# The high parts of the normed queries and keys are copied by GpSimd in place of ScalarE

## The reference

```
def rmsnorm(x, g):
    y = x32 * lax.rsqrt(jnp.mean(x32 * x32, axis=-1, keepdims=True) + NORM_EPS)
    return (y * g.astype(jnp.float32)).astype(x.dtype)
q = rmsnorm(split_heads(q, NSA_HEADS), q_g)         # NSA queries; keys ks, kw with k_g[1], k_g[2]
q = rmsnorm(split_heads(q, FOX_HEADS), q_g)         # FOX queries
k = rmsnorm(split_heads(k, FOX_HEADS), k_g)         # FOX keys
```

## Time and profile before

| | |
|---|---|
| median of 3 runs | 457.0 us (453.78 to 457.54) |
| the profiled execution, device time | 457.69 us |
| its span, first to last instruction | 455.9 us |
| busy: PE, DVE, ACT, POOL | 431.8, 297.0, 254.8, 74.4 us |
| mean granted TensorE clock | 0.981 of full speed |

### The profile page before, as it was taken

How to read it: one execution, slowest core, us unless ns; L and a number is a source line. 1 busy time by engine, 2 the same in 40 slices (tenths; PEclk the granted TensorE clock), 3 DMA queues, 4 the chain that set the end, 5 groups by cost and what they waited for, 6 DMA issues and landing times.

```text
span 455.9 us, 6481 instructions
## 1 busy us (share of the span) xinstructions
PE 431.8 (95%) x2205; PEld 332.8 (73%) x2205; DVE 297.0 (65%) x632; ACT 254.8 (56%) x500; POOL 74.4 (16%) x122
## 2 busy tenths in 40 slices
PE   5899999999589979999999999999799999999997
PEld 1477777878568866676667897888577778888885
DVE  5975569878858998767427873757886448722204
ACT  5645694766635577878618884852576635311100
POOL 4002240000000036666400000000166300000000
PEclk9899999999978999999999999999999999999999
DMA  7822404432041210000011224371400013832004
GB/s 250 330 92 93 128 13 126 109 99 93 0 138 48 92 47 3 1 1 1 1 46 48 93 74 158 103 214 55 138 2 1 1 46 106 294 110 92 0 1 184
DMA packets 12961, 39.15 MB, mean 86 GB/s; under 512 B 1792, under 2 KB 2048, under 8 KB 12672
## 3 DMA queue, kind: packets, MB, share of 16 engines
q1 hardware_dynamic: 12928, 38.73, 25.9%
HBM read 32.43 MB, written 2.10 MB: 76 GB/s over the span
## 4 chain that ended last, share of the span: by engine, by line
PE 79%; DVE 9%; ACT 6%; issue 3%; DMA 1%; SPq 1%; POOL 0%; DVEq 0%; ACTq 0%
PE bank L1185 11%; PE bank L1187 11%; PE bank L1186 11%; PE bank L1299 6%; PE bank L1280 6%; PE bank L1402 5%; PE bank L1400 5%; PE bank L1401 5%; PE bank L1271 3%; PE bank L1272 3%; PE bank L1196 2%; PE bank L1166 2%; PE bank L1215 2%; PE bank L1167 2%; PE bank L1168 2%
## 5 line engine op out<-in xcount | busy, mean ns | idle before, releaser
L1185 PE MATMUL bank<-xh,wh 128*128 128x512 f32 x256 | 110.0, 430 | 4.9 <-DVE wl L818 4.9
L1187 PE MATMUL bank<-xh,wl 128*128 128x512 f32 x256 | 102.0, 398 | 0.0
L1186 PE MATMUL bank<-xl,wh 128*128 128x512 f32 x256 | 101.4, 396 | 0.0
L818 DVE TENSOR_TENSOR wl<-raw,wh 128x1024 fp32r<-128x1024 f32 (+1 forms) x51 | 61.0, 1204 | 30.4 <-ACT wh L527 30.1
L527 ACT ACTIVATE wh<-raw 128x1024 fp32r<-128x1024 f32 (+1 forms) x51 | 52.3, 1036 | 30.2 <-PE bank L1402 29.6
L1185 PEld LDWEIGHTS bank<-xh,wh 128*128 128x128 f32 x256 | 49.2, 192 | 19.1 <-issue 9.7
L1186 PEld LDWEIGHTS bank<-xl,wh 128*128 128x128 f32 x256 | 49.0, 191 | 13.8 <-issue 4.0
L1187 PEld LDWEIGHTS bank<-xh,wl 128*128 128x128 f32 x256 | 49.0, 191 | 11.3
L1023 DVE CUSTOM_DVE_ANT_0 bank<-bank,mask_row 128x256 f32<-128x256 f32 (+3 forms) x96 | 46.7, 499 | 13.7 <-PE bank L1272 12.7
L490 POOL TENSOR_SCALAR probs<-probs,rcp,gates 128x384 f32<-128x384 f32 (+3 forms) x44 | 27.0, 624 | 118.1 <-DVE rcp L1039 118.0
L1402 PE MATMUL bank<-wh,yl 128*128 128x512 f32 x96 | 37.8, 394 | 0.0
(11 more groups left out here) (211 smaller groups left out, 782.3 us busy)
## 6 DMA issues: line engine op xcount, KB each, us to landing
raw<-in_w_in SPq DMA_DIRECT2D x36, 512.0 KB, 3.5
raw<-in_w_out SPq DMA_DIRECT2D x12, 512.0 KB, 3.4
x_raw<-in_xT SPq DMA_DIRECT2D x8, 256.0 KB, 5.9
x_res<-in_x_tok SPq DMA_DIRECT2D x1, 2048.0 KB, 9.4
out_y<-y_out SPq DMA_DIRECT2D x8, 256.0 KB, 2.1
raw<-in_w_in SPq DMA_DIRECT2D x3, 384.0 KB, 3.0
cmp_w_sb<-in_cmp_w SPq DMA_DIRECT2D x1, 1024.0 KB, 10.6
kh_fox<-kh_fox SPq DMA_DIRECT2D x8, 128.0 KB, 2.3
```

The costliest lines, as they stand in the source:

```text
L818: dve.tensor_tensor(wl[:, c % HL, cols], raw[:, c % RAW, cols], wh[:, c % HL, cols].bitcast(F32), ALU.subtract).then_inc(wl_ready, 1)
L1185: pe.matmul(dst, hi, xh[:, k, :], start=(k == 0), stop=False)
L1186: pe.matmul(dst, hi, xl[:, k, :], start=False, stop=False)
L1187: mm = pe.matmul(dst, lo, xh[:, k, :], start=False, stop=(k == KT - 1))
```

## The change

The 28 copies of high parts (two for each of the 14 normed chunks) leave ACT's queue and enter GpSimd's, from the same source to the same place. Each copy on GpSimd waits for `normed` of its chunk, for the recurrence's work on GpSimd, from fq 0 on for the 64 NSA scalings, and for the copy before it (`h_ready`). GpSimd's queue is written anew: the eight multiplications, the copies of the 6 chunks of NSA, the 64 scalings of NSA, the copies of the 8 chunks of FOX, the scalings of FOX. DVE's, PE's and SP's queues are unchanged, and wait for the same semaphores.

```diff
+            def norm_high(c):
+                kind, j = CHUNKS[c]
+                n = nth_normed(c)
+                pool.wait_ge(normed, n + 1)
+                if kind == "fq" and j == 0:
+                    pool.wait_ge(s_ready, NSA_UNITS)
+                for s in range(2):
+                    high, _ = operand_parts(c, s)
+                    pool.wait_ge(lru_ixs, LRU_T)
+                    if c >= NORMED[6]:
+                        pool.wait_ge(p_scaled, NSA_UNITS)
+                    if 2 * n + s:
+                        pool.wait_ge(h_ready, 2 * n + s)
+                    nc.gpsimd.tensor_copy(high, qr[half_of(s), n % 2, :]).then_inc(h_ready, 1)
...
+            for j in range(LRU_T):
+                pool.wait_ge(lru_sig, 2 * j + 2)
+                nc.gpsimd.tensor_tensor(ig[:, j, :], ig[:, j, :], xc[:, j, :], ALU.mult).then_inc(lru_ix, 1)
+            for j in range(LRU_T):
+                pool.wait_ge(lru_sqrt, j + 1)
+                pool.wait_ge(lru_ix, j + 1)
+                nc.gpsimd.tensor_tensor(ig[:, j, :], ig[:, j, :], u_pad[:, j, 0:SEQ], ALU.mult).then_inc(lru_ixs, 1)
+            for c in NORMED[0:6]:
+                norm_high(c)
+            pool.wait_ge(gates_ready, 1)
+            pool.wait_ge(h_ready, 12)
+            scale_probs(0, NSA_UNITS)
+            for c in NORMED[6:]:
+                norm_high(c)
+            pool.wait_ge(h_ready, 2 * len(NORMED))
+            scale_probs(NSA_UNITS, UNITS)
...
-            def norm_high(c):
...
-                        act.activation(high, qr[half_of(s), n % 2, :], ACT.Copy).then_inc(h_ready, 1)
...
-                    norm_high(c - 1)
...
-                norm_high(c - 1)
```

More of the change, by code:

```diff
@@ L491, in scale_probs @@
                                             ALU.mult, ALU.mult).then_inc(p_scaled, 1)
-            pool.wait_ge(small_consts, 1)
[L494 to L510, removed]
+            def norm_high(c):
[12 more added lines that the diff above has]
+                    nc.gpsimd.tensor_copy(high, qr[half_of(s), n % 2, :]).then_inc(h_ready, 1)
```

## The result

The changed kernel takes 460.77 us (median of 4 runs, 459.59 to 462.41) against 457.02 us (4 runs, 453.78 to 457.54): a ratio of 1.0095, 95% interval 1.0054 to 1.0136, or 2.5 to 6.2 us. The forecast was 461.6 us with a range of 457.0 to 467.0. The profiled execution took 459.59 us with a span of 457.4 us, against 457.69 and 455.9 us before.

The account below looks back on a forecast made before the run. The prediction took TensorE's matmuls as most of the time and DVE's queue as the bound up to zl 0; 3.93 us (NSA) plus 0.70 us (FOX) on the 457.0 us median gave 461.6 us, range 457.0 to 467 us.

Parts of the forecast that it names:

- The bound: From the norms of the NSA queries up to zl 0, DVE's queue bounds; it idles only 1.65 us in all there.
- ACT's relief is worth nothing: Taking 28 copies, 17.6 us, off ACT gains at most 0.37 us at the seeds for nq 2; counted at nothing.
- The copy: One GpSimd copy of 512 columns takes 0.65 us (0.52 to 0.77), bounded from memset, scaling and two-tensor product rows.
- The turns: GpSimd's second copy and DVE's first low part can't run at once, so the second low part starts 0.77 us later.
- rival 1: Second copy and first low part overlap, being on different partitions; 457.7 us, no difference; chance 0.19.
- d: Extra DVE time per normed chunk: 0.16 + 0.77 = 0.93 us, from 0.67 to 1.17 us with the copy's duration.
- The NSA stage: Six chunks delay DVE's queue before zl 0, less 1.65 us idle: zl 0 starts 3.93 us later (2.4 to 5.4).
- The FOX stage: Read-out of fk 0 comes 2.16 us late against 1.46 us slack before its square's mean: PE stalls 0.70 us.
- The clock: PE's restart at zl 0 may fall better or worse against the clock grant: 1.7 us either way, nothing in the sum.
- The sum: 3.93 + 0.70 = 4.6 us added to the 457.0 us median: 461.6 us, 1.0% slower.
- 2: Rival: the GpSimd copy is slow, 1.04 us or more, costing 11.6 us together: 468.6 us; chance 0.13.
- 3: Rival: faster, with memset-short copies, no turns and PE's restart sparing the half-clock slices: about 452 us; chance 0.04.

Follow-up runs that it names:

- the run without the chain: Changed kernel, but the second GpSimd copy of each chunk raises its own semaphore and no longer waits for the first's h_ready; one execution, 460.24 us.

## Why the prediction was right, and where it was off

**The bound.** Right. DVE's queue up to zl 0 was what the change lengthened, and a slip put into the old kernel brought PE's waits back at vn 2 and zl 0. The prediction missed two more idle spells of that queue, 0.60 us at 112.58 and 0.16 us at 115.18, both behind ACT ("nothing else"); they keep their length in the changed kernel, so they absorbed nothing and the sum isn't hurt.

**ACT's relief is worth nothing.** Right as far as these runs can tell: half of the copies off ACT without a turn gave 0.9981, with an interval that holds 1, and in the changed kernel PE gains more than 0.1 us nowhere but in half-clock stretches.

**The copy.** 0.65 us was taken, from 0.52 to 0.77 us; alone it takes 0.604 to 0.62 us. The two-tensor row's 0.62 us was the near one. The first low part was to be 0.16 us later; it is not: 0.70 us of idle time as with ACT. The two hand-offs of the earlier trace rows, 0.21 us, didn't belong there in full, since 0.70 less 0.61 leaves 0.09 us for both.

**The turns.** Right as a mechanism: the second copy is stretched from 0.61 to 1.04 us beside a low part and takes 0.62 us without one, with 64 partitions each and not the same ones, so rival 1's ground is gone. The size is the term that was off: +0.77 us was a whole copy with its hand-off after the low part, and it is 0.52 us, since the copy ends only 0.47 us behind the low part. So d = 0.52 us and not 0.93 us, below the lower end of 0.67 us. That the blocked copy has part of its work behind it when DVE is done was in none of my bounds.

**The NSA stage.** 3.93 us was forecast, 1.17 us measured (1.11 us with the NSA copies alone). The formula was sound: with 0.52 us it gives 6 x 0.52 - 1.65 = 1.47 us, and 0.80 us at the `wl` of vn 2, where the wait grew by 0.58 us. It was not paid twice, as said. Of the error of 2.8 us, 6 x (0.93 - 0.52) = 2.5 us is d. The other 0.3 us is that each of the three idle spells absorbed 0.07 to 0.1 us more than its length. An instruction of DVE that waits for nothing begins before the recorded end of the one ahead: the `wl` from 245.09 takes 1.22 us, and the read-out starts at 246.23.

**The FOX stage.** 0.70 us was forecast and 1.4 us measured (0.91 + 0.51 us in the changed kernel, 0.90 + 0.51 us with the copies of FOX alone), and this is the step whose mechanism was wrong. The prediction had PE wait for the square of fk 0, and said of vf 0 and vf 1 that the delay drains there. But a token-major chunk needs the `wl` of several chunks at once (`wait_ge(wl_ready, c + n)`), so the `wl` of vf 1 has to be there at the first matmul of vf 0, one chunk ahead and not three. In the kernel before it ended at 258.97 and PE went on at 259.02:

```profile
257.74 1.23 DVE L818 TENSOR_TENSOR wl<-raw,wh 128x1024 fp32r<-128x1024 f32 x1
```

```profile
259.02 0.39 PE L1166 MATMUL bank<-wh,xh 128*128 128x256 f32 x1
```

No slack, but no wait either, so no list of waits named it. From there the slip reaches PE whole: three pairs of 0.52 us, less two idle spells before read-outs that absorb 0.30 us each (0.21 us and the 0.09 us above), are 0.96 us, and 0.91 us is measured at vf 0. At vf 2 one pair alone, that of fk 1, stands between the last read-out for which DVE waited and the `wl` of vf 3: 0.52 us, 0.51 us measured. The wait for the square, with its slack of 1.46 us, stands right behind: it appeared when `split_low` was moved ahead. With the d that I had forecast, the same place would have cost 3 x 0.93 - 2 x 0.30 = 2.2 us.

**The clock.** The half-clock stretch behind zl 0 kept its 6.83 us, 0.3 us gained, within the 1.7 us allowed.

**The sum** came to 461.6 us against 460.77 us partly by luck. Two errors of opposite sign met, NSA 2.8 us too much and FOX 0.7 us too little, and the medians differ by 3.7 us where the traces give the change 1.2 + 0.9 + 0.5 = 2.6 us. The formula with the right d and the right places gives 1.5 + 1.0 + 0.5 = 3.0 us. Both lie within the interval of the measured loss, 2.5 to 6.2 us.

The rivals: 1 and 2 are refuted by the stretched second copy and by 0.61 us for a copy; 3, which needed a d below 0.1 us, by the 0.52 us.

## What to carry to other kernels

An engine that is idle is not free for work that feeds VectorE: ask what VectorE runs in the same moments. The same copy cost nothing when it ran in VectorE's idle time and 0.52 us per pair beside a subtraction of two SBUF operands; so split a pair over two idle engines that start together, and don't chain it on one. And before you call a delay absorbed, look for consumers that take several products at once, and compare the end of each producer with the start of its consumer: a slack of 0.05 us shows in no list of waits. When you imitate a delay by an added instruction, look where the time is lost before you believe the total: the one here matched the loss of the change, and some two thirds of it had another source.

## What the runs showed of the hardware

- Who goes first. In every pair the low part on DVE kept its 0.683 to 0.691 us, and the copy on GpSimd was stretched, also where the copy stood directly behind another and so began with the hand-off to DVE (1.14 us). By the earlier trace rows it had been DVE's instruction that was stretched. The Trainium skill, "SBUF — State Buffer", section "Who interferes with whom", says that the one that issues first has the shared ports for the whole instruction and the other blocks fully. In the run without the chain the second copy, the last 1.14 us of the piece from 243.01 that takes 1.81 us, starts at 243.68 and DVE at 243.65, so the trace agrees with the order.
- A blocked copy is not a copy that starts when the block ends. In all 14 chunks it ended 0.48 us after DVE's instruction, where a copy alone takes 0.61 us from its start: about 0.13 us of it, an estimate from these two, lie in the time in which it is blocked.
- The hand-off from GpSimd to DVE with a copy between them cost no more than that of ACT: 0.70 us of idle time for a copy of 0.61 us on the one and 0.63 us on the other.
- Half-clock stretches of PE at places that the change doesn't touch (3.41 us at 14.9 us in one execution, none in another) cost half their length, 1.7 us, as much as the effects of this study. Only the alignment behind them, or the medians, could be compared.
- PE's pace varies without any wait. The same 70 matmuls of vf 0 and vf 1 (from 263 to 271 us in the kernel before) stand 0.113 us apart in four of the executions and 0.118 us in eight, with the granted clock at its full level in all of them. Kernels with all copies on ACT are in both groups. One execution beside another tells less than 0.4 us there.
